# An opening in which each early adaLN chunk holds shift and scale of two feature blocks, and the chunks are taken between the blocks

## What is computed

```
ada = silu(c) @ w_ada + b_ada            # c: 9 condition rows (1 prompt, 8 samples), w_ada 1024 x 3072
shift, scale, gate = split(ada, 3)       # 1024 columns each
h = rmsnorm(x, norm_w) * (1 + scale) + shift
proj = h @ w_in                          # the mixer's input projection, q and f of head 0 first
```

## Time and profile before

| | before |
|---|---|
| time, median of three runs | 1120.97 us |
| the profiled execution's own time | 1122.75 us |
| its span | 1121.1 us |
| TensorE busy | 1089.2 us, 97% |
| VectorE busy | 635.8 us, 57% |
| ScalarE busy | 505.1 us, 45% |
| TensorE's granted clock, mean | 0.995 |

### The profile page before, as it was taken

How to read it: one execution, slowest core, us unless ns; L and a number is a source line. 1 busy time by engine, 2 the same in 40 slices (tenths; PEclk the granted TensorE clock), 3 DMA queues, 4 the chain that set the end, 5 groups by cost and what they waited for, 6 DMA issues and landing times.

```text
span 1121.1 us, 26202 instructions
## 1 busy us (share of the span) xinstructions
PE 1089.2 (97%) x11121; PEld 1038.6 (93%) x11121; DVE 635.8 (57%) x1280; ACT 505.1 (45%) x1035; POOL 151.0 (13%) x156
## 2 busy tenths in 40 slices
PE   8999999999999999998999999999999999999998
PEld 6799999999999998988998999999999999998997
DVE  3776676767585858673446634652455246437332
ACT  4653444445453545541124643653464365447122
POOL 1000010100000000000000730351045006300000
PEclk9999999999999999998999999999999999999999
DMA  9763444444544442219324455325623652263441
GB/s 321 282 206 110 142 134 149 137 144 128 153 126 147 134 136 77 81 52 273 104 76 142 117 134 152 100 71 118 166 77 97 152 138 80 60 156 87 152 113 47
DMA packets 232219, 147.73 MB, mean 132 GB/s; under 512 B 7876, under 2 KB 226206, under 8 KB 231591
## 3 DMA queue, kind: packets, MB, share of 16 engines
q1 hardware_dynamic: 217456, 134.17, 42.4%
q10 hardware_dynamic: 14646, 11.89, 3.2%
HBM read 124.00 MB, written 22.02 MB: 130 GB/s over the span
## 4 chain that ended last, share of the span: by engine, by line
PE 85%; DVE 6%; ACT 3%; issue 2%; DMA 2%; SPq 1%; ACTq 0%; DVEq 0%
PE PJ L382 26%; PE PJ L1707 18%; PE PJ L1415 15%; PE PJ L403 7%; PE X L1273 2%; PE X L1835 1%; PE X L1393 1%; PE X L1214 1%; PE X L1862 1%; PE PJ L685 1%; PE X L1395 1%; DMA pre<-in_ada_w_dram 1%; SPq L2521 1%; PE PJ L429 1%; PE X L1800 1%
## 5 line engine op out<-in xcount | busy, mean ns | idle before, releaser
L355 DVE TENSOR_TENSOR w_lo<-raw,w_hi 128x1024 fp32r<-128x1024 f32 (+1 forms) x128 | 157.0, 1239 | 163.0 <-ACT w_hi L347 162.1
L347 ACT ACTIVATE w_hi<-raw 128x1024 fp32r<-128x1024 f32 (+1 forms) x128 | 129.3, 1025 | 167.7 <-PE PJ L1707 69.9
L1707 PE MATMUL PJ<-w_hi,h_hi 128*128 128x256 f32 x600 | 167.3, 287 | 2.1 <-issue 1.4
L1707 PE MATMUL PJ<-w_lo,h_hi 128*128 128x256 f32 x600 | 164.6, 283 | 0.0
L382 PE MATMUL PJ<-h_hi,w_hi 128*128 128x288 f32 (+1 forms) x736 | 160.7, 300 | 0.6 <-ACT v_ L939 0.6
L382 PE MATMUL PJ<-h_hi,w_lo 128*128 128x288 f32 (+1 forms) x736 | 157.7, 296 | 0.0
L382 PE MATMUL PJ<-h_lo,w_hi 128*128 128x288 f32 (+1 forms) x736 | 157.4, 295 | 0.0
L1707 PE MATMUL PJ<-w_hi,h_lo 128*128 128x256 f32 x480 | 135.8, 283 | 0.0
L382 PEld LDWEIGHTS PJ<-h_hi,w_hi 128*128 128x128 f32 x736 | 118.1, 189 | 4.6 <-issue 3.1
L382 PEld LDWEIGHTS PJ<-h_hi,w_lo 128*128 128x128 f32 x736 | 118.9, 189 | 0.0
L382 PEld LDWEIGHTS PJ<-h_lo,w_hi 128*128 128x128 f32 x736 | 118.8, 189 | 0.0
(11 more groups left out here) (346 smaller groups left out, 2149.2 us busy)
## 6 DMA issues: line engine op xcount, KB each, us to landing
raw<-in_a_w_in_dram SPq DMA_DIRECT2D x48, 512.0 KB, 5.0
raw<-in_b_w_in_dram SPq DMA_DIRECT2D x64, 256.0 KB, 3.7
raw<-in_ada_w_dram SPq DMA_DIRECT2D x28, 512.0 KB, 3.9
kvc<-in_cache_kv_w_dram SPq DMA_DIRECT2D x24, 512.0 KB, 5.9
pre<-in_ada_w_dram SPq DMA_DIRECT2D x16, 512.0 KB, 10.1
s<-in_state_hgrn_dram SPq DMA_DIRECT2D x8, 1024.0 KB, 8.2
out_hgrn_sample_dram<-s ACTq DMA_DIRECT2D x8, 1024.0 KB, 5.0
raw<-in_a_w_out_dram SPq DMA_DIRECT2D x16, 512.0 KB, 5.0
```

Of the source, the lines that this page charges most:

```text
L347: act.activation(w_hi[:, i % SPLITS, 0:size], raw[:, n % RAWS, 0:size], ACT.Copy).then_inc(hi_done, 1)
L355: dve.tensor_tensor(w_lo[:, i % SPLITS, 0:size], raw[:, n % RAWS, 0:size], w_hi[:, i % SPLITS, 0:size].bitcast(F32), ALU.subtract).then_in ...
L1707: last = pe.matmul(PJ[:, tile // 2, tile % 2 * 256:tile % 2 * 256 + 256], a, b[:, k, :], start=(first and k == 0 and i == 0), stop=(kk == ...
```

## The change

The columns of the four chunks are dealt out anew. Chunk c now holds the shift and the scale of feature blocks 2c and 2c + 1, 256 columns each, loaded as four DMAs with runs of 1 KB. SP issues chunk 1 where chunk 2 was, and then chunks 2 and 3. TensorE multiplies chunk 0 after all transposes and turns it after the norm, multiplies chunk 1 before block 0 (now waiting for the root, since it uses a PSUM bank that the root is read from), and takes turn 1 after block 0, chunk 2 after block 1, turn 2 and chunk 3 after block 2, turn 3 after block 3. The filler matmuls are gone. VectorE makes amplitudes for two blocks at a time, four times, and its other work of the opening is dealt out between them. ScalarE copies the rows of chunks 1, 2 and 3 after blocks 0, 2 and 3. The four lower-bound operations stand behind `low(7)`. Further on only counts of two semaphores change (3 becomes 5).

```diff
-        FIRST_ADA = ((0, X[:, 2, :]), (2, PJ[:, 3, :]), (1, X[:, 2, :]), (3, X[:, 0, :]))
+        pairs_of = lambda x, p: x.rearrange("q (s m) n -> q s m n", s=2)[:, :, 2 * p:2 * p + 2]
+        FIRST_ADA = ((0, X[:, 2, :]), (1, X[:, 0, :]), (2, X[:, 2, :]), (3, X[:, 0, :]))
...
-        def turn_ada(rows, c, out):
+        def turn_ada(c):
+            rows, out = adr0[:, c], pairs_of(ada_t0, c)
             nc.tensor.wait_ge(adr_done, c + 1)
+            if c:
+                nc.tensor.wait_ge(ada_done, c)
...
-                if k == 5:
-                    pe.wait_ge(c_sb, 1)
-                    pe.wait_ge(par_done, 1)
-                    first_ada(0)
+            pe.wait_ge(c_sb, 1)
+            pe.wait_ge(par_done, 1)
+            first_ada(0)
             first_norm_pe(2)
             first_norm_pe(3)
             first_norm_pe(4)
...
+            turn_ada(0)
+            pe.wait_ge(n_r, 1)
             first_ada(1)
-            turn_ada(adr0[:, 0], 0, ada_t0[:, 0:4])
-            turn_ada(adr0[:, 2], 1, ada_t0[:, 8:12])
-            for _ in range(12):
-                pe.matmul(X[:, 2, 0:P], ones[:], ones[:], start=True, stop=True)
             for k in range(KD):
                 first_tickets(pe, k)
                 if k == 0:
+                    turn_ada(1)
+                if k == 1:
                     first_ada(2)
-                if k == 1:
-                    pe.wait_ge(n_r, 1)
+                if k == 2:
+                    turn_ada(2)
                     first_ada(3)
-                    turn_ada(adr0[:, 1], 2, ada_t0[:, 4:8])
-                    turn_ada(adr0[:, 3], 3, ada_t0[:, 12:16])
+                if k == 3:
+                    turn_ada(3)
...
-                act.wait_ge(amp_done, k // 4 + 1)
+                act.wait_ge(amp_done, k // 2 + 1)
...
-                act.wait_ge(n_hs, k // 4 + 1)
+                act.wait_ge(n_hs, k // 2 + 1)
                 act.activation(h_hi[:, k, 0:T], oz[:, k, :], ACT.Copy).then_inc(n_hx, 1)
-                if k == 3:
-                    first_ada_rows(act, 2, copy)
-                    first_ada_rows(act, 3, copy)
+                if k in (0, 2, 3):
+                    first_ada_rows(act, (1, 0, 2, 3)[k], copy)
...
+            amplitudes(0)
             dve.wait_ge(x_sb, KD)
             dve.wait_ge(n_r, 1)
+            scale_x(0)
...
-            first_ada_rows(dve, 1, dve.tensor_copy)
-            scale_x(0)
+            modulate_seqs(0)
             scale_x(1)
-            amplitudes(0)
-            scale_x(2)
             low(0)
             split_lo(("w", 0, 1))
             low(1)
+            scale_x(2)
             scale_x(3)
-            low(2)
-            scale_x(4)
-            scale_x(5)
-            low(3)
+            for p in range(1, 4):
+                amplitudes(p)
+                modulate_seqs(p)
+                low(2 * p)
+                if p < 3:
+                    scale_x(2 * p + 2)
+                low(2 * p + 1)
+                if p < 3:
+                    scale_x(2 * p + 3)
             dve.wait_ge(lb_exp, 1)
...
-            amplitudes(1)
-            scale_x(6)
-            scale_x(7)
-            for k in range(4, KD):
-                low(k)
...
             def first_ada_in(c):
-                for q in range(4):
-                    sp.dma_start(pre[:, 4 * c + q, :].rearrange("p (k c) -> p k c", k=2),
-                                 cols(adaw[0], 2 * q, 2, c * 512, 512)).then_inc(pre_in[c], 16)
+                chunk = pre[:, 4 * c:4 * c + 4, :].rearrange("p q (k c) -> p (q k) c", k=2)
+                for k0 in (0, 4):
+                    for x in range(2):
+                        sp.dma_start(chunk[:, k0:k0 + 4, x * 256:x * 256 + 256],
+                                     cols(adaw[0], k0, 4, x * D + c * 256, 256)).then_inc(pre_in[c], 16)
...
                 if n == 1:
+                    first_ada_in(1)
+                if n == 2:
                     first_ada_in(2)
-                if n == 2:
-                    first_ada_in(1)
                     first_ada_in(3)
```

More of the change, by code:

```diff
@@ L447, in first_ada_rows @@
             copy(adr0[:, c], src).then_inc(adr_done, 1)
-        def turn_ada(rows, c, out):
+        def turn_ada(c):
+            rows, out = adr0[:, c], pairs_of(ada_t0, c)
             nc.tensor.wait_ge(adr_done, c + 1)
+            if c:
+                nc.tensor.wait_ge(ada_done, c)
             for q in range(4):
-                last = nc.tensor.matmul(out[:, q, :], rows[:, q * P:(q + 1) * P], fold[:], start=True, stop=True)
+                last = nc.tensor.matmul(out[:, q // 2, q % 2, :], rows[:, q * P:(q + 1) * P], fold[:], start=True, stop=True)
             last.then_inc(adt_done, 1)
@@ L562, in second_norm_act @@
                     act.activation(late_adr, X[:, 3, :], ACT.Copy).then_inc(adr_done, 1)
-            act.wait_ge(n_hs, 3)
+            act.wait_ge(n_hs, 5)
             act.activation(h_hi[:, :, TP:T], xa[:, :, TP:T], ACT.Copy).then_inc(n_hx, 1)
@@ L727, in low, with amplitudes, modulate_seqs @@
                 dve.tensor_tensor(h_lo[:, k, :], oz[:, k, :], h_hi[:, k, 0:T].bitcast(F32), ALU.subtract).then_inc(n_lo, 1)
[L729 to L736, removed]
+            def amplitudes(p):
+                dve.wait_ge(adt_done, p + 1)
+                bias = adab[:, 0, 0:2 * KD].rearrange("q (s m) -> q s m", s=2)[:, :, 2 * p:2 * p + 2]
+                dve.tensor_tensor(pairs_of(ada[:, 0, 0:2 * KD], p), pairs_of(ada_t0, p),
+                                  bias.unsqueeze(3).to_broadcast([P, 2, 2, NC_]), ALU.add).then_inc(ada_done, 1)
+                dve.wait_ge(ada_done, p + 1)
+                make_amp(0, 2 * p, 2 * p + 2)
+            def modulate_seqs(p):
+                k0, k1 = 2 * p, 2 * p + 2
+                dve.wait_ge(amp_done, p + 1)
                 xs = oz[:, k0:k1, TP:T].rearrange("p k (b t) -> p k b t", b=DB)
-                by = lambda x: x.unsqueeze(3).to_broadcast([P, 4, DB, DS])
+                by = lambda x: x.unsqueeze(3).to_broadcast([P, 2, DB, DS])
                 chain(dve.tensor_tensor(xs, xs, by(amp[:, k0:k1, 1:]), ALU.mult))
@@ L2678, in _ @@
             make_amp(1, 0, KD)
-            dve.wait_ge(amp_done, 3)
+            dve.wait_ge(amp_done, 5)
             dve.wait_ge(unparked, 16)
```

## The result

The changed kernel takes 1126.09 us (median of five, 1125.18 to 1128.68) against 1120.73 (median of five, 1120.45 to 1121.94): a ratio of 1.0049, 95% interval 1.0035 to 1.0064, so 5.4 us slower. The forecast was +1.1. The profiled execution took 1126.09 us with a span of 1124.4, 3.3 us over the span before. Its marks against the trace before: the `q_` product of head 0 is 3.0 us late (55.65 against 52.64), TensorE's ticket 4 2.4 us (72.56 against 70.14), the `q_` products of heads 3 and 7 2.4 us (146.67 and 422.47 against 144.30 and 420.07). The rest comes near 480 us.

The account below looks back on a forecast made before the run. TensorE, 97% busy, bounds the kernel; the opening's last half is TensorE's. Block 0's 1.4 us gain becomes 1.0 lost by block 7, +1.1 at `v_`: span 1122.2, forecast 1122.1 us against the 1120.97 median, range 1119.4 to 1124.8.

Parts of the forecast that it names:

- The root and block 0: Opening: root ready at 26.3, about half a microsecond earlier; TensorE starts block 0 at 31.47 instead of 32.84, 1.4 us earlier.
- the 1 KB runs: Chunk loads ahead of the second weight: shorter runs cost 0.29 us a chunk, from a 369 GB/s row, within 0 to 1.4.
- The serial tail: End of the opening: ScalarE's and VectorE's order delays blocks 6 and 7, turning 1.4 us won into 1.0 lost.
- Block 6's wait: TensorE, late in the opening: 1.5 us idle before block 6, which starts at 50.29.
- ticket 2: TensorE, behind the opening's feature blocks: starts at 55.04 instead of 53.45, +1.6 us.
- the opening as a whole: Opening up to the `v_` wait, which ends at 71.2 instead of 70.14: a loss of 1.1 us.
- Rival 1, the clock: TensorE's 3.2 us gap before block 0: clock falls to half, losing 2.5 us, total +3.6, 1124.6 us; chance 0.17.
- a premise against it: Trace before: gaps up to 2.1 us left the clock full, and 3.2 us is nearer to these than to 5.2.
- Removed: 12 filler matmuls that ran beside waiting, worth nothing unless the clock falls: TensorE, opening: taking out the fillers (24 instructions in the records) changes no time unless the clock falls.
- Later heads repeat what they did: Heads after the opening: run as before, with no term of their own beyond the opening's +1.1 us.

Follow-up runs that it names:

- e6: The changed kernel with VectorE's small operations, scale_x and amplitudes(3) moved earlier, and fillers back (6 before, 12 after chunk 1's matmuls): 1121.18 us, 1.0000 of the kernel before.
- e2: The kernel before with its four chunks loaded in 1 KB runs, four feature blocks of rows per DMA instead of two: 1123.55 us, ratio 1.0017.
- e1: The changed kernel with filler matmuls back, 6 ahead of chunk 1's matmuls and 12 between those and block 0: 1123.67 us, 1.0018 of the kernel before.
- e10: The kernel before with 12 matmuls fewer: 3 wide fillers replace its 12, and 9 warm-up matmuls replace 12; 1123.45 us, ratio 1.0019.
- e3: The kernel before without its 12 filler matmuls ahead of block 0: 1124.59 us, ratio 1.0029.
- e8: The kernel before with its 12 fillers replaced by 12 one-column matmuls on 32 weight columns: 1121.92 us, ratio 1.0005.
- e7: The changed kernel with 12 one-column matmuls on 32 weight columns added behind chunk 1's matmuls: 1124.51 us, 1.0028 of the kernel before.
- e5: The changed kernel with VectorE's lower-bound operations, scale_x and amplitudes(3) moved earlier, no fillers: 1125.21 us, 1.0033 of the kernel before.
- e9: e6 with the second weight loaded ahead of chunk 1, and 12 fillers, all ahead of chunk 1's matmuls: 1120.88 us, 0.9996 of the kernel before.

## Why the prediction was wrong

- *The root and block 0.* Right in its number, 31.55 against 31.47, by luck in part. TensorE's first transposes of `x` started at 8.69, in the trace before at 9.30, and this head start hid that the 1 KB runs cost 0.6 and not 0.29 us a chunk; in e6, where they started at 8.97, block 0 came at 31.95. The price was taken from the nearest row, and the term was half of what it is. In the kernel before the longer loading alone is worth 1.9 us (e2). The Trainium skill ("DMA: Bandwidth & Descriptors", Specifications), with line rate from 512 B on, does not fit these rows: the stretches in 1 KB runs moved at 348 and 369 GB/s and the one in 2 KB runs at 387.
- *The serial tail.* Right in place, and in size as far as the uncertainty tells. Block 6's wait was 1.61 (1.5 forecast), ticket 2 in e1 at 54.98 (55.04), and with the clock held mark 3 is 0.85 us late (e1), where the opening as a whole was to lose 1.1. Undoing the order gives 2.0 us with an uncertainty of 1.4 (e6 against e1), where the same working gave 1.0 to 1.8; by mark 3 it is 0.8.
- *Rival 1, the clock.* It happened, another way than I priced it. I looked for an idle gap of 3.2 us behind chunk 1's matmuls; it fell before that gap, in a stretch where TensorE had only the 9-column turn, a wait and matmuls on 32 weight columns. Its cost in the opening is about 1.5 us by mark 3 (after against e1), where I had 2.5. It deserved more than 0.17, for a premise against it was misread. The prediction says that the gaps up to 2.1 us left the clock full, but behind the one of 2.12 us the same trace has it at 0.50 (timeline of TensorE, then a window):

```profile
...
446.62 3.26 PE L1273 MATMUL X<-v_,kr 128*128 128x256 f32 x8 [2.12 <-ACT kr L943]
...
```

```profile
...
448.00:450.00 2.00, 2.00 (x8) 1.62 (x6) 0.00 (x0) 0.00 (x0) 0.00 (x0) 0.50 0.00 0
...
```

  The other eleven traces have the same wait (2.12 or 2.13 us) with the clock at 1.00 behind it, so the length of a gap alone does not tell whether the clock falls.
- *The step that failed:* "Removed: 12 filler matmuls that ran beside waiting, worth nothing unless the clock falls", with "Later heads repeat what they did". The fillers were also instructions. Taking 12 of them out moved the burst near 480 us onto a second place where TensorE's instruction supply runs dry, for +2.1 us with the clock held (e10), 2.7 by e3 against e8 and 2.4 by after against e7. No term of the sum stood for it, and by its middle value it is the largest single one.
- *The account*, by the ratios: the removed fillers 3.5 us (after less e1), of which the instruction supply is 2.1 to 2.7 and the clock about 1.1 (e7 less e1); VectorE's order 2.0 (e1 less e6); the rest, the new layout with its earlier start, its extra turn and its shorter runs, 0.0 (e6 against the kernel before). Together 5.5. A ratio to the kernel before is uncertain by 1.0 to 1.6 us, a difference of two such ratios by 1.4 to 2.0. So the clock's 1.1 is not shown by the times, only by mark 3 (1.5 us) and the granted clock; that the parts add up so well is luck.

That the instruction supply is what runs dry is the name that fits all rows. A 16 KB load on the instruction queue at 480 to 481 us would say little alone, for such loads stand all along (before at 471.6, 477.0 and 483.2 us, after at 476.9, 480.4 and 486.7), but the waits stand 256 instructions apart in the stream and each ends 2.2 to 2.7 us behind the start of a load. The Trainium skill ("Runtime: NRT & Kernel Launch", Instruction fetch mechanics) has instructions refilled in 16 KiB blocks of 256, and calls the cost mostly hidden; the size agrees with the 0.02 MB packet and the distance with the 128 records, the hiding does not hold in this burst. In the trace before, the place with 5652 records ahead is reached at 475.7, 4.1 us behind the start of a load; in the trace after at 477.9, 1.0 us behind one. Why the load starts so late there stays open.

## What to carry to other kernels

A matmul that computes nothing may hold the clock and may also set where the instruction stream is refilled: before removing or adding some, look for bursts of small matmuls with an "issue" wait anywhere later in the trace, and test with the same number of near-empty instructions. When work that came in one step is cut into four, follow it to the last step: a head start at the front is lost if the last quarter's small operation stands behind another's wait. Compare marks (one event per head) between two traces before explaining a difference in spans, as they tell at once where time was lost.

## What the hardware showed that I had not expected

- A second wait of 1.5 to 2.1 us on TensorE near 480 us that comes and goes with 12 matmuls 450 us earlier (e3 1.53, after 2.12, e5 1.85, e10 1.80 us; none in e7, e8), and that stands at the same count of instructions in every kernel.
- The clock fell to 0.50 during chunk 1's matmuls (27.5 us), with TensorE busy 1.13 of the 2 us before, and in e3 at 30.5, 1.2 us into a gap of 3.29 us. With twelve one-column matmuls in the fillers' place it fell as well (e7, e8), with twelve of 128 columns it stayed at 1.00 (e9 and before).
- The same wait of 2.12 us near 446 us was followed by a clock of 0.50 in one trace of twelve (before).
- Loads of 1 KB runs from the 12 KB rows of `w_ada` moved at 348 GB/s, the 1 KB stretch at 66 us of the trace before at 369.
